# Scores of the first two pairs of heads ahead of the gates and value tiles, with PSUM banks given out anew, in a two-block kernel

## What is computed

```python
z = rms_norm(x, attn_norm) @ w_in                 # a_conv, q, kc, vc, ks, vs, kw, vw, g
conv_out = silu(layer_norm(conv31(u * sigmoid(v)) + b))
kc, vc = compress(kc), compress(vc)               # 15 compressed keys and values a group
gates = sigmoid(g)                                # tokens x 12 heads x 3 branches
o_c = softmax(q @ kc - alibi, mask) @ vc
o_s = softmax(q @ ks - alibi, mask) @ vs          # 256 tokens: all of their blocks are taken
o_w = softmax(q @ kw - alibi, mask) @ vw
nsa = g0 * o_c + g1 * o_s + g2 * o_w
x = x + concat(conv_out, nsa) @ w_out             # then a gated feed-forward
```

## Time and profile before

| | |
|---|---|
| runs of the kernel before | 788.24, 791.12, 793.45 us (median 791.12) |
| the profiled execution | 790.49 us, of it span 788.7 us |
| PE busy | 748.8 us (95%) |
| DVE busy | 545.6 us (69%) |
| ACT busy | 377.7 us (48%) |
| granted TensorE clock, mean | 0.989 |

### The profile page before, as it was taken

The page is one execution under the profiler, slowest core; times in us unless marked ns, Lnnn a source line. Parts: engine busy times, 40 slices in busy tenths (PEclk is TensorE's granted clock), DMA queues, the critical chain, the costliest instruction groups (busy, mean ns, idle before and its releaser), DMA issues.

```text
span 788.7 us, 13263 instructions
## 1 busy us (share of the span) xinstructions
PE 748.8 (95%) x5370; PEld 690.8 (88%) x5370; DVE 545.6 (69%) x888; ACT 377.7 (48%) x516; POOL 53.3 (7%) x72
## 2 busy tenths in 40 slices
PE   5999987989999999997999999999997999999996
PEld 5999975779999999996999989899887999999985
DVE  6796878356467777696669968775867786545554
ACT  6432868444434333435545346665436443444342
POOL 2940000000000000030231000000000000000000
PEclk9999999999999999999999999999998999999999
DMA  8637502027778887942554456554532765446511
GB/s 325 210 120 261 215 4 105 15 92 284 260 277 309 326 292 293 359 149 107 187 207 154 168 170 225 198 187 187 168 152 89 271 228 190 173 170 213 198 69 53
DMA packets 27019, 151.06 MB, mean 192 GB/s; under 512 B 3128, under 2 KB 7836, under 8 KB 9564
## 3 DMA queue, kind: packets, MB, share of 16 engines
q1 hardware_dynamic: 22620, 124.81, 44.2%
q10 hardware_dynamic: 3456, 25.17, 8.2%
q0 software_dynamic: 896, 0.43, 0.2%
HBM read 148.92 MB, written 1.05 MB: 190 GB/s over the span
## 4 chain that ended last, share of the span: by engine, by line
PE 79%; DVE 13%; ACT 3%; issue 3%; DMA 1%; SPq 0%; DVEq 0%; ACTq 0%
PE ps L418 24%; PE ps L419 24%; PE ps L420 24%; DVE ada L1438 3%; DVE w_lo L1340 2%; ACT w_hi L974 1%; PE ps L524 1%; DMA raw<-wts 1%; PE ps L848 1%; DVE ada L1507 1%; PE ps L589 1%; DVE ada L1579 1%; DVE soft L1507 1%; PE ps L482 1%; PE ps L790 0%
## 5 line engine op out<-in xcount | busy, mean ns | idle before, releaser
L1340 DVE TENSOR_TENSOR w_lo<-raw,w_hi 128x2048 fp32r<-128x2048 f32 (+1 forms) x111 | 251.1, 2269 | 125.3 <-ACT w_hi L974 125.1
L418 PE MATMUL ps<-h_hi,w_hi 128*128 128x256 f32 x1064 | 306.0, 288 | 7.0 <-DVE h_lo L1391 3.2
L419 PE MATMUL ps<-h_lo,w_hi 128*128 128x256 f32 x1064 | 303.5, 285 | 0.0
L420 PE MATMUL ps<-h_hi,w_lo 128*128 128x256 f32 x1064 | 303.2, 285 | 0.0
L974 ACT CAST w_hi<-raw 128x2048 fp32r<-128x2048 f32 (+1 forms) x111 | 207.7, 1885 | 62.2 <-PE ps L420 55.6
L418 PEld LDWEIGHTS ps<-h_hi,w_hi 128*128 128x128 f32 x1064 | 205.3, 193 | 11.4 <-issue 6.6
L419 PEld LDWEIGHTS ps<-h_lo,w_hi 128*128 128x128 f32 x1064 | 205.4, 193 | 1.5 <-issue 0.2
L420 PEld LDWEIGHTS ps<-h_hi,w_lo 128*128 128x128 f32 x1064 | 205.2, 193 | 0.3
L418 PE MATMUL ps<-w_hi,mix_hi 128*128 128x512 f32 x248 | 97.4, 393 | 1.1 <-DVE mix_lo L1612 1.1
L419 PE MATMUL ps<-w_lo,mix_hi 128*128 128x512 f32 x248 | 96.8, 390 | 0.0
L420 PE MATMUL ps<-w_hi,mix_lo 128*128 128x512 f32 x248 | 96.5, 389 | 0.0
(11 more groups left out here) (259 smaller groups left out, 860.7 us busy)
## 6 DMA issues: line engine op xcount, KB each, us to landing
raw<-wts SPq DMA_DIRECT2D x113, 1024.0 KB, 4.8
ada<-w_ada ACTq DMA_DIRECT2D x24, 1024.0 KB, 5.3
resid<-x SPq DMA_DIRECT2D x2, 512.0 KB, 3.7
raw<-wts SPq DMA_DIRECT2D x2, 512.0 KB, 6.7
rows_ga<-rows_wide SPq DMA_DIRECT2D x1, 1024.0 KB, 7.4
out<-resid SPq DMA_DIRECT2D x4, 256.0 KB, 2.0
shared<-shared SPq DMA_DIRECT2D x2, 320.0 KB, 6.8
raw<-w_idx SPq DMA_DIRECT2D x1, 544.0 KB, 3.3
```

What stands on the lines that cost most here:

```text
L418: nc.tensor.matmul(o, lh, rh, start=start, stop=False)
L419: nc.tensor.matmul(o, lh, rl, start=False, stop=False)
L420: return nc.tensor.matmul(o, ll, rh, start=False, stop=stop)
L1340: V.tensor_tensor(w_lo[:, s % RING, 0:w], raw[:, n_of[name] % RAW, 0:w], w_hi[:, s % RING, 0:w].bitcast(F32), ALU.subtract).then_inc(w_rea ...
```

## The change

On PE, scores(0) moves to just behind the convolution's mean, ahead of compress(1), and scores(1) to behind the gate tile. The turns of heads 0 and 1 leave the loop: they come behind vw, ahead of pcT, which now also waits for the copies of head 1; late_keys(0) follows. In the loop, which starts at j = 1, late_keys(1) comes before values(0). On DVE, masked(0) and masked(1) come behind the convolution's mean, ahead of the vw split; normal(0), masked(2) and normal(1) ahead of the k1 split and the compressed softmax; masked(3) and the out0 split behind it. On ACT, attn(0) and attn(1) come ahead of vw's cast; the copy-out of vs behind the convolution's silu, then attn(2), the compressed exponential, out0's cast, vw's copy-out. In the loops ACT does attn(n+3) in place of attn(n+2), with k1's copy-out ahead of it, and DVE masked(n+3) and normal(n+2).

Banks: g 7, vs 6, vw 7, k1 7, mean and variance 6, second layers 4 and 5, the turned gates 7. probs[2] and probs[3] move from the tensor `ada` to `rows_ga`.

```diff
-VW_BANK, K1_BANK = 6, 7
+OWN_BANK = {"g": 7, "vs": 6, "vw": 7, "k1": 7}
...
-        probs = [soft[:, 0:768], soft[:, 768:1536], early[:, 0:768], early[:, 768:1536]]
+        probs = [soft[:, 0:768], soft[:, 768:1536], rows_ga[:, 0, 0:768], rows_ga[:, 1, 0:768]]
...
-            pe.wait_ge(z_evac, s_idx["vw"])
-            pe.wait_ge(lnv_ready, 1)
-            scores(0)
-            slot, _ = project_1(s_idx["vw"])
-            token_tile(slot, VW_BANK, h_hi, h_lo, 0, T, T).then_inc(pe_tile, 1)
-            pe.wait_ge(s_sb, 8)
-            scores(1)
...
+            def own_bank(name):
+                pe.wait_ge(w_ready, s_idx[name] + 1)
+                return s_idx[name] % RING, OWN_BANK[name]
+
+            compress(0)
...
+            i.then_inc(conv_mean, 1)
+            pe.wait_ge(z_evac, s_idx["k0"] + 1)
+            scores(0)
+            compress(1)
...
+            slot, bank = own_bank("g")
+            narrow_tile(slot, ps[0:G_COLS, bank, 0:T], 0, G_COLS, G_COLS).then_inc(pe_tile, 1)
+            pe.wait_ge(s_sb, 8)
+            scores(1)
...
+            pe.wait_ge(lnv_ready, 1)
+            token_tile(*own_bank("vs"), h_hi, h_lo, 0, T, T).then_inc(pe_tile, 1)
+
+            pe.wait_ge(vblk_ready, NQ)
+            pe.wait_ge(cmp2_sb, 2)
...
+            pe.wait_ge(z_evac, s_idx["g"] + 1)
+            token_tile(*own_bank("vw"), h_hi, h_lo, 0, T, T).then_inc(pe_tile, 1)
+
+            pe.wait_ge(sc_sb, 1)
+            for n in range(2):
+                probs_turn(n)
             pe.wait_ge(pc_ready, 1)
+            pe.wait_ge(pTn_ready, 4)
             for c in range(3):
...
             i.then_inc(pcT_ps, 1)
-
-            pe.wait_ge(vblk_ready, NQ)
-            pe.wait_ge(pcT_ready, 3)
             pe.wait_ge(z_evac, s_idx["vw"] + 1)
-            for j in range(NQ // 2):
-                if 1 <= j < NQ // 2 - 1:
+            late_keys(0)
+
+            for j in range(1, NQ // 2):
+                if j + 1 < NQ // 2:
                     pe.wait_ge(s_sb, 8 * (j + 1))
                     if j == 2:
                         pe.wait_ge(z_evac, s_idx["k1"] + 1)
                     scores(j + 1)
+                if j == 1:
+                    pe.wait_ge(pcT_ready, 3)
                 probs_turn(2 * j)
-                if j >= 1:
-                    values(j - 1)
-                probs_turn(2 * j + 1)
-                if j == 0:
-                    late_keys(0)
                 if j == 1:
                     late_keys(1).then_inc(pe_tile, 1)
+                values(j - 1)
+                probs_turn(2 * j + 1)
             values(NQ // 2 - 1)
```

On ACT:

```diff
             nc.scalar.copy(xs_cmp(0), ps[:, 4, 0:264]).then_inc(cmp_sb, 1)
+            attn(0)
+            attn(1)
             after(7)
...
             after(8)
-            copy_out(s_idx["vs"])
-            after(9)
             act.wait_ge(lnn_ready, 1)
...
+            copy_out(s_idx["vs"])
+            attn(2)
             act.wait_ge(sc_sb, 1)
             nc.scalar.activation(scmp, scmp, ACT.Exp).then_inc(pc_exp, 1)
...
-            attn(0)
-            attn(1)
+            after(9)
             copy_out(s_idx["vw"])
...
-                if n + 2 < NQ:
-                    attn(n + 2)
+                if n == 3:
+                    copy_out(s_idx["k1"])
+                if n + 3 < NQ:
+                    attn(n + 3)
                 if n == 1:
                     after(s_idx["vw"])
-                if n == 3:
-                    copy_out(s_idx["k1"])
```

On DVE:

```diff
+            masked(0)
+            masked(1)
             after(7)
...
+            dve.wait_ge(z_evac, s_idx["g"] + 1)
+            normal(0)
+            masked(2)
+            normal(1)
+            after(8)
...
             V.tensor_tensor(scmp, scmp, wide(mx), ALU.subtract).then_inc(sc_sb, 1)
-            masked(0)
-            masked(1)
...
-            normal(0)
+            masked(3)
+            after(9)
...
             for n in range(NQ):
+                if 1 <= n < NQ - 3:
+                    dve.wait_ge(pT_ps, 2 * n)
+                    masked(n + 3)
                 if n + 2 < NQ:
-                    if n >= 2:
-                        dve.wait_ge(pT_ps, 2 * (n - 1))
-                    masked(n + 2)
-                if n + 1 < NQ:
-                    normal(n + 1)
+                    normal(n + 2)
```

More of the change, by code:

```diff
@@ L526, in compress @@
                     i.then_inc(direct_done, 1)
[L528 to L556, removed]
             def head_at(h):
@@ L565, in qT @@
                 return z[b:b + HD, Q0 + j // 2, (j % 2) * T:(j % 2 + 1) * T]
[L568 to L577, removed]
             order = [6 * p + r + 3 * e for p in range(2) for r in range(3) for e in range(2)]
@@ new lines, in _ @@
+            compress(0)
+            pe.wait_ge(s_const, 16)
+            pe.wait_ge(conv_ready, 1)
+            for c in range(2):
+                i = nc.tensor.matmul(ps[:, 6, 0:T], cst("mean"), conv[:, c, :], start=(c == 0), stop=(c == 1))
+            i.then_inc(conv_mean, 1)
+            pe.wait_ge(z_evac, s_idx["k0"] + 1)
+            scores(0)
+            compress(1)
+            pe.wait_ge(convd_ready, 1)
+            for c in range(2):
+                i = nc.tensor.matmul(ps[:, 6, T:2 * T], cst("mean"), lnq[:, c, :], start=(c == 0), stop=(c == 1))
@@ new lines, in _ @@
+            i.then_inc(conv_var, 1)
+            slot, bank = own_bank("g")
+            narrow_tile(slot, ps[0:G_COLS, bank, 0:T], 0, G_COLS, G_COLS).then_inc(pe_tile, 1)
+            pe.wait_ge(s_sb, 8)
+            scores(1)
+            pe.wait_ge(s_w2, 16)
+            pe.wait_ge(cmp_h, 2)
+            for f in range(2):
+                i = nc.tensor.matmul(ps[0:HD, 4, 0:P], w2[:, 0, f, :], hcmp[0][:, f, :], start=(f == 0), stop=(f == 1))
+            i.then_inc(cmp2_ps, 1)
+            pe.wait_ge(cmp_h, 4)
@@ new lines, in _ @@
+            for f in range(2):
+                i = nc.tensor.matmul(ps[:, 5, 0:HD], hcmp[1][:, f, :], w2[:, 1, f, :], start=(f == 0), stop=(f == 1))
+            i.then_inc(cmp2_ps, 1)
+            pe.wait_ge(narrow_sb, 1)
+            for m in range(2):
+                i = nc.tensor.transpose(ps[:, 7, T + m * HD:T + m * HD + G_COLS], gT[:, m * P:(m + 1) * P], ident[0:G_COLS, 0:G_COLS])
+            i.then_inc(narrow_ps, 1)
+            pe.wait_ge(lnv_ready, 1)
+            token_tile(*own_bank("vs"), h_hi, h_lo, 0, T, T).then_inc(pe_tile, 1)
@@ new lines, in _ @@
+            pe.wait_ge(vblk_ready, NQ)
+            pe.wait_ge(cmp2_sb, 2)
+            for m in range(2):
+                for h in range(NQ):
+                    _, b, _ = head_at(h)
+                    g = h // 3
+                    at = ((2 * m + h // 6) * 3 + h % 3) * CMP_SLOT
+                    i = nc.tensor.matmul(ps[:, 4 + b // HD, at:at + CMP_SLOT], qT(h)[:, m * P:(m + 1) * P],
+                                         kcmp[b:b + HD, g * CMP_SLOT:(g + 1) * CMP_SLOT], start=True, stop=True)
@@ L1034, in copy_out @@
                 name = s_name[s]
-                bank = {"vw": VW_BANK, "k1": K1_BANK}.get(name, s % 3)
+                bank = OWN_BANK.get(name, s % 3)
                 if name == "g":
@@ L1051, in _, with attn @@
                     after(s)
+            def attn(n):
+                act.wait_ge(s_sb, 4 * (n + 1))
+                for br in range(2):
+                    for m in range(2):
+                        o = probs[n % 4][:, br * 384 + m * P:br * 384 + P + m * T]
+                        c = 2 * br + m
+                        nc.scalar.activation(o, o, ACT.Exp, scale=-1.0, bias=nmax[:, n % 2, c:c + 1],
+                                             accum_out=psum_p[:, n % 2, c:c + 1]).then_inc(p_exp, 1)
             act.wait_ge(direct_done, 2)
             nc.scalar.copy(xs_cmp(0), ps[:, 4, 0:264]).then_inc(cmp_sb, 1)
+            attn(0)
+            attn(1)
             after(7)
@@ L1066, in _ @@
                 nc.scalar.copy(kcmp[b * HD:(b + 1) * HD, :].rearrange("p (g n) -> p g n", g=NKV),
-                               ps[0:HD, 6, 0:P].rearrange("p (g n) -> p g n", g=NKV)[:, :, 0:CMP_SLOT]).then_inc(cmp2_sb, 1)
+                               ps[0:HD, 4, 0:P].rearrange("p (g n) -> p g n", g=NKV)[:, :, 0:CMP_SLOT]).then_inc(cmp2_sb, 1)
             act.wait_ge(narrow_ps, 1)
-            nc.scalar.activation(gates, ps[:, s_idx["g"] % 3, T:T + 2 * HD].rearrange("p (m c) -> p m c", m=2)[:, :, 0:G_COLS].rearrange(
+            nc.scalar.activation(gates, ps[:, 7, T:T + 2 * HD].rearrange("p (m c) -> p m c", m=2)[:, :, 0:G_COLS].rearrange(
                 "p m (h b) -> p m h b", b=3), ACT.Sigmoid).then_inc(z_evac, 1)
@@ L1470, in compressor_sum @@
                 i.then_inc(cmp_sum, 1)
[L1472 to L1493, removed]
             order = [6 * p + r + 3 * e for p in range(2) for r in range(3) for e in range(2)]
@@ L1525, in nsa_lo @@
                 V.tensor_tensor(mix_lo[:, 2 + j, :], ps[:, 6 + j % 2, 0:T], mix_hi[:, 2 + j, :].bitcast(F32), ALU.subtract).then_inc(o_lo, 1)
```

(22 more changed lines are left out.)

4 lines of the change are left out of this document (2 added, 2 removed).

## The result

The changed kernel takes 798.19 us (median of 5 runs, 796.17 to 801.44), the kernel before 791.19 (5 runs). The ratio is 1.0093, with a 95% interval from 1.0055 to 1.013: about 7.4 us slower. The forecast was 795.0 with a range to 799. The sign and the range held; the slowdown is nearly twice the 4.2 us forecast, two of the five runs (801.34 and 801.44) lie above the range, and the loss of 0.93% is just inside the 1% that got a chance of 0.89. The profiled execution took 801.34 us (span 799.5).

What follows compares the result with a forecast made beforehand. ACT and DVE were taken to bind the loop over heads, PE almost level. Terms 1.2 + 0.5 + 0.2 + 2.0 = 3.9, plus 0.3 for latencies, gave +4.2 us: 795.0 us, range 788.5 to 799.

Steps and rivals of the forecast that it cites:

- Steps 1 to 3: Early scores and attn cost 0; bank waits nothing, or 0.3 us; on DVE the compressed softmax's first part ends 4.3 later.
- Step 4: ACT behind the compressed softmax: scores(2) start at 110.7 us against 110.49, so three heads ahead bought nothing for them.
- Step 5: ACT at n = 1: attn(4) ahead of out1's cast and head 2's copies, idle 7.6 us; scores(3) +1.2 (0.2 to 2).
- Steps 6 and 7: Loop: pairs 5.9 us apart, +0.5, and +0.2 over the out2 split; tail from scores(5) to out tiles +2.0.
- the paragraph on the clock behind the sum: Sparse stretch ahead of late_keys(0) grows from 4 us to 100.9 to 106.8; by the transposes rule late_keys(0) runs low throughout.
- Rival C: Low clock throughout: late_keys(0), scores(2) and work behind two gaps slowed; 4.2 + 4.7 = 8.9 us, 799.5; chance 0.07.
- Rival A: Work in front pays: ACT's loop loses 5.3 us; 4.6 off, 786; right if scores(2) before 108.5; chance 0.20.

Runs made afterwards that it cites:

- filled kernel: The changed kernel with 23 spare matmuls, results unused, in TensorE's longest waits (turns 0 and 1, before scores(3), turn(7), turn(10)); ratio 1.0043 to the kernel before.
- one edit: The changed kernel with out1's cast moved ahead of attn(4) on ACT at n = 1; ratio 1.0074 to the kernel before.
- two-ahead runs: The changed kernel with its loop put back to two heads ahead (1.0033); also with scores(2) directly behind turn(1) and out0's cast before the compressed exponential (0.9954).
- two ahead, mended: The changed kernel with its loop back at two heads ahead, scores(2) directly behind turn(1), out0's cast before the compressed exponential; ratio 0.9954 to the kernel before.

## Why the prediction was half right

The measured 10.4 us between the two profiles (94.95 - 84.59) part as follows; "order" is the kernel with filled gaps less the kernel before, "clock" the rest.

| interval | forecast | measured | order | clock |
|---|---|---|---|---|
| c-s2 | +0.2 | +2.41 | +0.10 | +2.31 |
| s2-s3 | +1.0 | +0.68 | +0.59 | +0.09 |
| s3-s4 | +0.5 | +2.39 | +0.74 | +1.65 |
| s4-s5 | +0.2 | +0.32 | +0.33 | 0 |
| s5-out | +2.0 | +4.56 | +1.97 | +2.59 |
| sum | 3.9 | 10.36 | 3.73 | 6.63 |

The split is not quite even-handed, since the kernel before has low clock of its own behind the first turns, where the filled kernel has none. With the 1.33 us that filling gave back there in the kernel before, c-s2 parts into +1.43 for order and +0.98 for clock, and the sum into about 5.1 and 5.3. These are estimates from single profiles, and spare matmuls push too: pcT starts 46.18 us behind compress(0) in the filled kernel, 45.79 in the changed one. What the low clock in scores(0) and vw costs the kernel before, no run shows, for both profiles of its order, filled or not, have it.

*Steps 1 to 3* (front, banks, DVE's order) came out as priced: attn(0) and attn(1) in ACT's idle, the table load behind the wait, the compressed scores ready for their exponential at about 100.4 against a forecast of 99.7. *Step 4* had scores(2) at 110.7, and in the filled kernel they come 49.80 us behind compress(0), which is 110.6 on that scale; but that is in part luck. The 110.7 has late_keys(0) at 3.9 us, partly at low clock, and the filled kernel needs 3.0; what made up for it is pcT, which starts at 106.84 in the changed kernel and not at 105.9. The claim that the early front buys nothing for them is right. *Step 5* is right in mechanism (one edit gave back 1.6 us) and in size. *Steps 6 and 7* are right in size: 0.74, 0.33 and 1.97 for 0.5, 0.2 and 2.0, and with the loop two ahead they vanish. What PE waits for before turns 7 and 10 is DVE's normal, where step 7 had ACT's copy of head 9 as the last.

**What failed is the paragraph on the clock behind the sum**, and the price it left at that of the kernel before. The order term was 3.9 and measured 3.7 to 5.1, as the low clock of the kernel before is counted; the clock term was taken as unchanged and measured 5.3 to 6.6 in the profiled execution. By the ratio the kernel is 7.4 us slower where the profile is 10.8 (spans 799.5 and 788.7). Three of the five executions have a mean granted clock of 0.982 to 0.984 against the profiled one's 0.980, so they lose less to it. That the range held is luck as well: its upper end, 799, was made of the bounds of steps 5 and 7 and the spread of runs, with nothing for the clock. Rival C had this mechanism, with 4.7 us for it, and I gave it 0.07, because the kernel before stayed at 1.00 behind gaps of 2.14 and 2.25 us. That was one execution of one order. The two-ahead runs have the same gap of 2.25 us and a fall behind it, and so has the kernel before itself, once its earlier gaps are filled. The Trainium skill's sentence on transposes ("TensorE: Matmul & The Clock Gate", Part 4) spoke for C. The changed kernel's first stretch agrees with it, low through nearly all of late_keys(0) (5.2 us for 24 matmuls, where the filled kernel needs 3.0), but no run here separates transposes from plain idleness.

Rival A fell at its own test: scores(2) were not before 108.5. Its premise holds, though: ACT's idle could be put to use, once scores(2), out0's cast and the loop were placed so that ACT didn't stand at attn(4) with ready work behind it (ratio 0.9954).

## What to carry to other kernels

Giving an in-order engine its work earlier pays only if nothing queued behind it is needed sooner: here the depth of the lookahead put exponentials that needed new scores ahead of copies and a cast that were ready. Take the front of such a change without the deeper loop, and put ready work (here scores(2) and out0's cast) into the waits. Where a change opens gaps or stretches of sparse work on TensorE, price them twice, once as waiting and once as the following matmuls at half clock, and don't take one profile's full clock behind a gap as a promise.

## What the runs showed of the hardware

In the changed kernel the clock fell behind gaps of only 2.1 to 2.7 us, in four stretches of 3.4 to 7 us, at places that repeated within 0.5 us in two executions. In the kernel before it fell behind two gaps of 1.23 and 1.08 us beside the turns, and behind 2.25 us it stayed at 1.00; with its earlier gaps filled it fell behind those 2.25 us. So in this case the length of a gap alone doesn't tell whether the clock falls. It also fell, in nine of the thirteen profiled executions, in vw or just ahead of it, where PE had no gap at all, behind 48 small matmuls of 16 columns (two ahead, mended: 4 us, PE busy throughout):

```profile
93.50:97.50 4.00, 4.00 (x23) 4.00 (x23) 3.93 (x8) 3.99 (x10) 0.00 (x0) 0.57 0.02 4
```

In the other four, the changed kernel's first among them, it didn't. Why stays open.
